# Computing block 0 from expert 0's tokens of tiles 0 to 3, in plain fp32, while the other tokens are still being routed

## The reference

```python
    s = jax.nn.sigmoid((xf @ w_router).astype(jnp.float32))
    sb = (s + router_bias).reshape(T, N_GROUPS, EXPERTS_PER_GROUP)
    group_score = lax.top_k(sb, 2)[0].sum(-1)
    gsel = jnp.argmax(group_score, axis=-1)
    ...
    counts = jnp.bincount(flat_e, length=N_EXPERTS)
    padded = (counts + MOE_BLOCK - 1) // MOE_BLOCK * MOE_BLOCK
    ...
    def expert_block(args):
        xblk, e = args
        return (jax.nn.silu(xblk @ w1[e]) * (xblk @ w3[e])) @ w2[e]
```

## Time and profile before

| | |
|---|---|
| time, median of 3 runs | 888.96 us (888.73 to 889.39) |
| time of the profiled execution | 889.26 us |
| its span, first to last instruction | 887.5 us |
| PE busy | 858.4 us (97%) |
| DVE / ACT / POOL busy | 636.0 / 414.9 / 192.3 us |
| mean granted TensorE clock | 0.986 |
| HBM traffic | 195.29 MB, 220 GB/s |

### The profile page before, as it was taken

How to read it: one execution, slowest core, us unless ns; L and a number is a source line. 1 busy time by engine, 2 the same in 40 slices (tenths; PEclk the granted TensorE clock), 3 DMA queues, 4 the chain that set the end, 5 groups by cost and what they waited for, 6 DMA issues and landing times.

```text
span 887.5 us, 14102 instructions
## 1 busy us (share of the span) xinstructions
PE 858.4 (97%) x4980; PEld 706.4 (80%) x4981; DVE 636.0 (72%) x907; ACT 414.9 (47%) x597; POOL 192.3 (22%) x225
## 2 busy tenths in 40 slices
PE   8999999999999999999799999999999999999993
PEld 6789878888997567887688888888888888888872
DVE  1578755789777748556985669399936648599995
ACT  3585456201224442222343456378634525487772
POOL 4042001100000101011032324133413222234324
PEclk9999999999999999999979999999999999999997
DMA  9953566511035032322789859979997596599994
GB/s 342 347 180 111 172 196 203 163 41 54 11 143 191 1 143 78 113 73 95 259 304 375 277 171 368 285 269 378 378 346 265 176 299 220 175 348 379 370 333 175
DMA packets 82358, 195.29 MB, mean 220 GB/s; under 512 B 4919, under 2 KB 13324, under 8 KB 82314
## 3 DMA queue, kind: packets, MB, share of 16 engines
q1 hardware_dynamic: 71168, 158.87, 50.2%
q0 software_dynamic: 8272, 25.84, 11.2%
q10 hardware_dynamic: 2874, 10.01, 2.9%
HBM read 169.57 MB, written 25.71 MB: 220 GB/s over the span
## 4 chain that ended last, share of the span: by engine, by line
PE 78%; DVE 11%; DMA 4%; issue 2%; ACT 2%; POOL 1%; ACTq 0%; SPq 0%; DVEq 0%; POOLq 0%
PE ps L2455 17%; PE ps L2443 12%; PE ps L2108 9%; PE ps L2460 8%; PE ps L2111 7%; PE ps L2437 2%; PE ps L2308 2%; DMA raw<-in_w_dram 2%; PE ps L2299 1%; DMA raw<-x_rows 1%; DVE arena L1423 1%; PE ps L2301 1%; PE ps L2300 1%; PE ps L2250 1%; PE ps L2164 1%
## 5 line engine op out<-in xcount | busy, mean ns | idle before, releaser
L1145 ACT ACTIVATE wah<-raw 128x2048 fp32r (+1 forms) x32 | 61.4, 1919 | 63.7 <-PE ps L2460 42.4
L1856 DVE TENSOR_TENSOR wbl<-raw,wbh 128x2048 fp32r<-128x2048 f32 x32 | 73.1, 2288 | 5.3 <-ACT wbh L1145 4.9
L2443 PE MATMUL ps<-w2h,hTh 128*128 128x512 f32 x184 | 76.1, 414 | 0.0
L2455 PE MATMUL ps<-wbh,xTh 128*128 128x512 f32 x184 | 73.9, 402 | 0.0
L2455 PE MATMUL ps<-wah,xTh 128*128 128x512 f32 x184 | 72.6, 394 | 0.0
L2443 PE MATMUL ps<-w2h,hTl 128*128 128x512 f32 x184 | 72.2, 393 | 0.0
L2455 PE MATMUL ps<-wal,xTh 128*128 128x512 f32 x184 | 72.2, 392 | 0.0
L776 POOL DMA_INDIRECT x_rows<-late_rows,block_dst x21 | 49.9, 2375 | 102.7 <-DVE late_rows L1871 102.7
L2443 PE MATMUL ps<-w2l,hTh 128*128 128x512 f32 x184 | 72.1, 392 | 0.0
L1856 DVE TENSOR_TENSOR wal<-raw,wah 128x2048 fp32r<-128x2048 f32 x30 | 68.8, 2292 | 4.5 <-issue 3.2
L1856 DVE TENSOR_TENSOR w2l<-raw,w2h 128x2048 fp32r<-128x2048 f32 x32 | 71.8, 2283 | 0.0
(11 more groups left out here) (412 smaller groups left out, 2173.8 us busy)
## 6 DMA issues: line engine op xcount, KB each, us to landing
raw<-in_w_dram SPq DMA_DIRECT2D x64, 1024.0 KB
raw<-in_w_dram SPq DMA_DIRECT2D x16, 2048.0 KB, 11.3
arena<-in_w_mod_dram SPq DMA_DIRECT2D x32, 512.0 KB, 4.0
arena<-in_x_dram SPq DMA_DIRECT2D x16, 512.0 KB, 9.5
arena<-in_w_mod_dram SPq DMA_DIRECT2D x3, 2048.0 KB, 13.9
arena<-in_w_in_dram SPq DMA_DIRECT2D x6, 1024.0 KB, 7.1
x_rows<-arena ACTq DMA_DIRECT2D x9, 512.0 KB, 3.0
hx_rows<-arena ACTq DMA_DIRECT2D x9, 512.0 KB, 4.5
```

The costliest lines, as they stand in the source:

```text
L1145: act.activation(high_half, raw_half, ACT.Copy).then_inc(w_high[j], 1)
L1856: dve.tensor_tensor(low_half, raw_half, high_half.bitcast(F32), ALU.subtract).then_inc(w_split[j], 1)
L2443: ins = pe.matmul(out_ap, parts[l][:, lhs], w_parts[w][:, cols], start=start and n == 0, stop=stop and n == 2)
L2455: pe.matmul(ps[:, 2 + j, :], xTh[:, k * P:(k + 1) * P], w[:, k * HALF:(k + 1) * HALF], start=(k == 0 and w is wh), stop=False)
```

## The change

- On DVE `choose(0, FIRST)` moves from iteration 7 to iteration 6, and `early_sums` (two small additions), `early_places` and `early_tokens` are added; they give the places and the token list of expert 0's tokens of tiles 0 to 3.
- On PE `early_ranks` (two small matmuls) stands in iteration 7 between `project_pooled` and `project_gated(6, 0)`, `early_list` (four) behind `turn_outputs(7)`, and `turn_early` (eight transposes) in iteration 8 ahead of `turn_normed(6, 1)` and the last `project_gated`. POOL gathers the rows into `x_early` during iteration 8.
- `room_e` (128 less the number of these tokens) is added to the ranks of expert 0's later tokens, so that they start in block 1.
- Block 0's products with w1 and w3 are 16 plain fp32 matmuls from `raw`: twelve behind the ranks of all tokens and ahead of the token list, four behind the list. Its w2 products are 8 plain fp32 matmuls, with `turn_block(1)` between the halves. The block loop begins at 1.
- All `keep_busy` calls in the routing go.
- The slot weights are summed with operands exchanged (32x128 results in four row groups, then one matmul with `sel_b`).
- SP's load of expert 1's first unit waits for the gather of block 1, its third for block 0's last product.

```diff
+            def early_sums():
+                mine = R["sel"][:, :, 0]
+                v(dve.tensor_tensor(R["two_of"][:, 0, :], mine[:, 1:8], mine[:, 0:7], ALU.add))
+                dve.tensor_tensor(R["four_of"][:, 0, :], R["two_of"][:, 0, 0:5], R["two_of"][:, 0, 2:7], ALU.add).then_inc(S["route_ready"], 1)
...
+                if t == NX - 2:
+                    v(dve.memset(R["sel"][:, 0:4, :], 0.0))
+                    early = choose(0, FIRST)
+                    next(early)
                 if t == NX - 1:
                     clear_counts()
-                    early = choose(0, FIRST)
-                    next(early)
...
-                if t == NX - 1:
+                if t == NX - 2:
                     for _ in early:
                         pass
+                    early_sums()
+                if t == NX - 1:
+                    early_tokens()
...
+            dve.wait_ge(S["silu_done"], 2)
+            dve.wait_ge(S["l1c"], 1)
+            dve.tensor_tensor(hid[:, :], hsil[:, :], ps[:, 4, :], ALU.mult).then_inc(S["hid_a"], 1)
...
+            def early_ranks():
+                pe.wait_ge(S["on_ready"], 2 * (NX - 1))
+                pe.wait_ge(S["route_ready"], 1)
+                pe.matmul(ps[:, 2, 256:261], ones[:, :], rt["four_of"][:, 0, :], start=True, stop=False)
+                pe.matmul(ps[:, 2, 256:260], strict[:, :], rt["sel"][:, 4:8, 0], start=False, stop=True).then_inc(S["rank_done"], 1)
...
+            def turn_early():
+                pe.wait_ge(S["gathered"], 16)
+                for k in range(KC):
+                    ins = pe.transpose(ps[:, k // 4, (k % 4) * P:(k % 4 + 1) * P], x_early[:, k * P:(k + 1) * P], ident[:, :])
+                ins.then_inc(S["x_turned"], 1)
+
+            def early_product(unit, s_):
+
+                columns = raw[:, (unit + 1) * UNIT:(unit + 2) * UNIT].rearrange("p (k s n) -> p k s n", k=4, s=2)
+                for k in range(4):
+                    ch = 4 * unit + k
+                    ins = pe.matmul(ps[:, 2 + 2 * s_, :], xT_e[:, ch * P:(ch + 1) * P], columns[:, k, s_, :], start=(ch == 0), stop=(ch == KC - 1))
+                return ins
...
                     project_pooled(t - 1, 0)
                     if t >= 2:
                         project_pooled(t - 1, 1)
+                    if t == NX - 1:
+                        early_ranks()
                     project_gated(t - 1, 0)
...
                 if 2 <= t <= NX:
                     turn_normed(t - 2, 0)
+                if t == NX:
+                    turn_early()
...
-            keep_busy(20)
-
+            pe.wait_ge(S["tok_ready"], 1)
+            pe.wait_ge(w_loaded[0], LOADS[0])
+            early_product(0, 0)
+            pe.wait_ge(S["small_ready"], 3)
+            early_product(0, 1)
+            pe.wait_ge(w_loaded[1], LOADS[1])
+            early_product(1, 0).then_inc(S["l1a"], 1)
             for n in range(2 * NX):
...
             ins.then_inc(S["rank_done"], 1)
+            early_product(1, 1).then_inc(S["l1c"], 1)
...
+            for h in range(2):
+                for k in range(4):
+                    ins = pe.matmul(ps[:, 6 + h, :], hT_e[:, k * P:(k + 1) * P], rows_w2[:, k, h * HALF:(h + 1) * HALF], start=(k == 0), stop=(k == 3))
+                ins.then_inc(S["l2_done" if h else "l2_half"], 1)
+                if h == 0:
+                    turn_block(1)
```

More of the change, by code:

```diff
@@ L62 @@
 NGR = 4
-MAXB = 31
-NB = MAXB + 1
+MAXB = 32
+NB = MAXB
 UNIT = KC * HALF
@@ L616, in load_expert @@
                         sp.sem_inc(S["load_seen"], 1)
+                    if first and n == 5:
+                        sp.wait_ge(S["l2_done"], 1)
                     if not (first and turn == 0):
@@ L754, in _ @@
                     pool.wait_ge(S["pow_ready"], NT + u + 1)
+                if t == NX - 1:
+                    for par in range(2):
+                        pool.wait_ge(hx2_stored[par], 16 * 2)
+                    pool.wait_ge(S["tok_ready"], 1)
+                    pool.indirect_dma_start(out=x_early, out_offset=None, in_=hx_dram[0:4 * P, :],
+                                            in_offset=bass.IndirectOffsetOnAxis(ap=block_tok[:, :], axis=0))\
+                        .then_inc(S["gathered"], 16)
             for par in range(2):
@@ L798, in end_roots @@
                 end_power(t, n)
-            gather(0, False)
+            gather(1, False)
             pool.wait_ge(S["tok_table"], 1)
@@ L1174, in arrived @@
                 act.sem_inc(S["load_seen"], 1)
-            turn_out(0)
+            turn_out(1)
             act.wait_ge(S["table_ready"], 1)
             last = act.value_load(tabs[0:1, T_LAST:T_LAST + 1], min_val=NE - 1, max_val=MAXB - 1)
+            e, word = entry(act, 0)
+            with act.If(word > NE - 1):
+                place = [place_of(e, j) for j in range(3)]
+                arrived(0, e)
+                arrived(1, e)
+                for j in range(2):
+                    for k in range(2):
+                        act.wait_ge(w_split[j], k + 1)
+                        act.sem_inc(S["load_seen"], 1)
+                        high(j, place[k] * UNIT, k)
+                arrived(2, e)
+                for k in range(2):
+                    act.wait_ge(w_split[2], k + 1)
+                    act.sem_inc(S["load_seen"], 1)
+                    high(2, place[2] * UNIT, k)
             def block(b):
@@ L1213, in _ @@
             with act.Fori(0, NB // 4) as four:
-                i = four * 4
+                i = four * 4 + 1
                 with act.If(i < last):
@@ L2403, in _ @@
                     turn_outputs(t)
+                if t == NX - 1:
+                    early_list()
                 if t >= 2:
```

151 lines of the change are left out of this document (109 added, 42 removed).

## The result

The changed kernel takes 899.74 us, the median of 5 runs (897.98 to 900.23), against 889.13 us for the kernel before in the same session: a recorded ratio of 1.0114, with a 95% interval of 1.0099 to 1.0129 (the two medians alone give 1.0119). It is 1.1% slower, some 7 us beyond the range of the prediction. The profiled execution took 900.23 us, its span is 898.5 us, 11.0 more than before.

The account below looks back on a forecast made before the run. PE was taken as the bound, through the start of block 1. A gain of 4.3 us at full clock and 4.4 us of clock loss summed to +0.1, giving 889.1 us; range 885.8 to 892.8.

Parts of the forecast that it names:

- whatever moves the start of block 1 moves the end by the same amount: Expert stage: only PE's matmuls set the pace from block 1 to the last block, so block 1's start decides.
- signs of being wrong: Listed: full clock through the twelve products, DVE's early signal, a late weight unit, or block 1 waiting for DVE's low parts.
- The hole at `early_ranks`: Iteration 7: PE idles 4.0 us for DVE's choice, plus 0.5 us for two small matmuls; PE +4.5 us.
- The likeliest case: Whole kernel: gains and losses meet, 889.1 us, own range 887.3 to 890.6; chance 0.40.
- the third case: Tile loop: the `early_ranks` hole halves the clock, costing 1.7 us, then 2.5 in the twelve products; 890.8 to 893.3; chance 0.25.
- The early gather: Iteration 8: block 0's rows land 4.6 us after the gather begins; PE idles 3 us ahead of `turn_early`.
- (c): Behind the gather wait: half clock on the last gated product and its neighbours, +1.6 us.
- (a): Block 0: half clock through the first 4.6 us of the twelve products, +2.3 us.
- (b): Routing: half clock through about 1 us of small matmuls, +0.5 us.
- Ranks to products: Routing: ranks end at 445.3, twelve products take 10.3 us at full clock, the list 2.0 and waits for PE.
- Block 0's second half: From `block_tok` at 458.1 through hidden rows and w2 products to block 1's start at 473.0, full clock.
- Weights: Loads start at 435.9; second unit there by 453.0, third by 460.6; taken at nothing, 1 us if the second is late.

Follow-up runs that it names:

- lows_spread: Changed kernel with expert 1's low parts back between block 1's hidden rows on DVE, expert 0's w2 low parts ahead of block 1: 892.28 us.
- spin_hole: Changed kernel with 16 idle fp32 products on a constant matrix ahead of PE's wait at the early ranks: 896.74 us.
- before_nobusy: Kernel before without its three `keep_busy` calls: 892.95 us, ratio 1.0039.
- all_busy: all_three with 12, 4 and 2 idle products ahead of three PE waits (late choice, hidden rows, their transposed copy): 881.27 us.
- all_three: Changed kernel with early ranks and choice pieces in existing gaps, block 0's row transposes in the late-choice wait, and lows_spread's order: 882.36 us.
- list_first: all_busy with the token list behind eight of block 0's products instead of twelve: 879.24 us.
- lows_first: Changed kernel with only expert 0's w2 low halves moved ahead of block 1's hidden rows on DVE: 900.06 us.
- before_choice: Kernel before with only the choice for tiles 0 to 3 moved ahead of tile 7's masks: 891.36 us, ratio 1.0018.

## Why the prediction was wrong

**The bound, and where the sum stopped.** The step that failed worst is the first one: "whatever moves the start of block 1 moves the end by the same amount", repeated as "from there blocks as before". The earlier trace rows showed that for the kernel before. The change rewrites DVE's list of block 1 and part of block 2, and what those lines do to the blocks behind was left out of the costing: `first_low(1)`, two `low` and `turn_out(1)` were followed to the start of block 1, and no further. The 6.7 us between block 1's and block 3's starts came from there, and lows_spread, which changes DVE's order there and nothing else, gives 7.5 us back. It is most of the error of 10.6; block 1 itself started 4.1 us later than the sum had it. The prediction named the right engine among its signs of being wrong (block 1 waiting for DVE's low parts), but put no term on it, and the wait came one block later.

**The hole at `early_ranks`.** Its length was right: 4.0 us forecast, 3.94 measured, released by DVE. The term for PE was +4.5, and `outputs(7)` started 8.2 us late; the difference is the clock behind the hole (0.4 us of it was there before the hole). The likeliest case had kept the clock whole at this place; the third case, at 0.25, had it fall, and that mechanism is what happened. Its number, 890.8 to 893.3, meets lows_spread's 892.28 partly by luck: its first term, 1.7 us behind the hole, measured 3.0; its second, 2.5 us for a later return in the twelve products, did not come; and the w2 products' 1.7 us, below, was in no case. Rows at both levels were at hand, and a hole of 4 us in dense work is longer than the gaps of 1.2 us and less that had brought the clock down before. The Trainium skill's page "TensorE: Matmul & The Clock Gate", section "What's actually happening", says that the throttled state is the default, which activity releases. The traces agree in both directions: spin_hole keeps the clock at 1.00 over the same wait of useful work, and before_nobusy leaves it at 0.50 for 23 us and more.

**The early gather.** Landing in 4.4 us against 4.6, a wait of 2.26 against 3: right, and (c), half clock on the last gated product and its neighbours, was +1.6 and measured +1.5 (4.88 us from the start of `turn_normed(6, 1)` to the router, against 3.35). With the first hole's clock the residual came 10.5 us late, not 6.2 plus 1.6.

**Ranks to products.** (a) was right: 10.3 + 2.3 us forecast for the twelve products, 12.5 measured (450.67 to 463.17). (b) was +0.5, and the last ranks alone, at half clock, took 1.9 us against 0.9. The list took 2.1 us against 2.0 and waited for PE, not for DVE, as forecast.

**Block 0's second half.** Forecast from `block_tok` to the first product of block 1, with hand-offs: 14.9 us (458.1 to 473.0); measured 15.5 (466.0 to 481.5). The w2 products ran into the fourth stretch at half clock, which cost them about 1.7 us (5.37 against 3.60) and was not in the sum; everything else in this part took about 1.1 us less than forecast, so the near match is luck.

**Weights** were taken at nothing, and no product waited for them in this trace. That also was luck. The second unit was there at 458.52, 18.2 us after issue at 440.30, and its first product started at about 459.7 (an estimate: four products, 3.44 us, back from 463.17), late as it was by the half clock. In all_busy, at full clock, PE waited 0.80 us for that unit, near the 1 us that the prediction allowed for it.

**The range** left out the worst of the third case, and no case held a loss behind block 1's start.

**What the change is worth** where its parts stand well: the mechanism of the 4.3 us won was real and larger. With its holes closed block 1 starts 10.0 us (all_three) to 11.6 us (list_first) earlier than before, and the end comes 8.2 to 10.5 us earlier by the ratios. The exchanged operands of the slot weights and the plain fp32 products were not tested by themselves.

## What to carry to other kernels

Where a change rewrites an engine's list, follow that engine to the point where its list is word for word the old one, not to the end of the stage that was meant; here the loss lay two blocks later, on an engine that was 71% busy. A hole in the middle of dense matmul work costs its length and then the clock behind it, three quarters as much again here (3.0 us behind 3.94); so work that feeds an early step belongs into gaps that the feeding engine has already, in pieces if need be. A wait that stays can be filled, with transposes and list products first and with idle products where there are none. What that gives depends on what PE meets next: 3.0 us in spin_hole, 1.1 in all_busy, where the weights were then the bound.

## What the runs showed of the hardware

The clock can fall without a long hole: in the changed kernel it fell at 472.8 behind some 2 us of matmuls on 128 columns and fewer, with 1.06 and 0.59 us of idling among them. It does not do so each time: all_three has the same work and the same two waits at that place and kept 1.00 there, and so did lows_first. all_busy, with those waits filled, kept 1.00 too; whether the thin work or the short waits matter more was not separated. Behind the wait for the gather, 2.26 us in otherwise dense work, the clock fell as well, and behind 2.33 us in before_choice.

The same hole also cost different stretches at half clock in different executions (6.8 us from 408.0 in the changed kernel, 3.4 us from 408.8 in lows_first, whose PE list is the same there). That may be part of why lows_first and lows_spread scatter over 3.5 and 4.8 us and the two kernels with the busy waits over 1.2, but it is not shown: the changed kernel itself scatters over 2.3, and before_nobusy, with the longest stretch at half clock of all, over 0.8.
